# One ring of weight pieces 4096 bytes apart, instead of six buffers 4160 bytes apart

## The reference

```python
for l in range(DEPTH):
    h = rmsnorm(x, pre_norm_g[l])
    proj = h @ w_in[l]                      # 1024 x 10,432
    ...
    merged = (sigmoid(g_a) * (y_a @ w_proj_a[l]) + sigmoid(g_b) * (y_b @ w_proj_b[l])
              + sigmoid(g_c) * (y_c @ w_proj_c[l]))
    x = x + rmsnorm(merged @ w_out[l], post_norm_g[l])
# second block, per layer: pooling or sparse attention, then
    u = h @ w_up                            # 1024 x 5632
    x = x + (silu(g) * a) @ w_down          # 2816 x 1024
    x = x + sigmoid(rmsnorm(x) @ ple_gate[i]) * (p[i] @ ple_proj[i])
```

## Time and profile before

| | |
|---|---|
| median of 3 runs | 1482.29 us (1480.97 to 1482.8) |
| the profiled execution, its own time | 1483.7 us |
| its span, first to last instruction | 1481.9 us |
| TensorE busy | 1437.0 us, 97% |
| TensorE weight loads | 1292.4 us, 87% |
| VectorE busy | 1055.7 us, 71% |
| ScalarE busy | 871.8 us, 59% |
| mean granted TensorE clock | 0.988 of full speed |

### The profile page before, as it was taken

How to read it: one execution, slowest core, us unless ns; L and a number is a source line. 1 busy time by engine, 2 the same in 40 slices (tenths; PEclk the granted TensorE clock), 3 DMA queues, 4 the chain that set the end, 5 groups by cost and what they waited for, 6 DMA issues and landing times.

```text
span 1481.9 us, 23062 instructions
## 1 busy us (share of the span) xinstructions
PE 1437.0 (97%) x9283; PEld 1292.4 (87%) x9283; DVE 1055.7 (71%) x1601; ACT 871.8 (59%) x1522; POOL 85.2 (6%) x138
## 2 busy tenths in 40 slices
PE   8999999999999999999999999999999999999997
PEld 8988999788789989897887789998799888999886
DVE  7736669886666456698876778884676645888746
ACT  7464766564454657575644656664674543766645
POOL 9100000007000000000000000000000000000000
PEclk9999999999999999999999999999999989999999
DMA  8614476556556244765665446665535003666553
GB/s 256 187 47 150 132 225 196 173 186 198 191 144 173 76 144 120 214 186 175 193 220 184 157 132 215 207 205 187 170 103 159 29 1 106 206 186 188 190 178 114
DMA packets 189210, 240.98 MB, mean 163 GB/s; under 512 B 19086, under 2 KB 133954, under 8 KB 189104
## 3 DMA queue, kind: packets, MB, share of 16 engines
q1 hardware_dynamic: 183232, 228.66, 50.7%
q0 software_dynamic: 5776, 10.82, 2.4%
q10 hardware_dynamic: 96, 0.03, 0.0%
HBM read 238.42 MB, written 1.05 MB: 162 GB/s over the span
## 4 chain that ended last, share of the span: by engine, by line
PE 82%; DVE 8%; ACT 5%; DMA 2%; issue 2%; SPq 0%; DVEq 0%
PE bank L620 24%; PE bank L623 23%; PE bank L624 23%; DVE w_lo L1874 2%; PE bank L837 2%; PE bank L1216 2%; ACT w_hi L1321 1%; DMA raw<-in_w_in 1%; ACT T L1815 1%; DMA raw<-in_mla_w_ukv 1%; DMA raw<-in_w_out 1%; DVE rec L1998 1%; PE bank L1173 1%; PE bank L1130 1%; PE bank L1202 1%
## 5 line engine op out<-in xcount | busy, mean ns | idle before, releaser
L1874 DVE TENSOR_TENSOR w_lo<-raw,w_hi 128x1024 fp32r<-128x1024 f32 (+2 forms) x452 | 520.5, 1172 | 240.3 <-ACT w_hi L1321 236.6
L1321 ACT CAST w_hi<-raw 128x1024 fp32r<-128x1024 f32 (+2 forms) x452 | 450.8, 1008 | 271.5 <-DMA raw<-in_w_in 113.4
L620 PE MATMUL bank<-h_hi,w_hi 128*128 128x256 f32 (+1 forms) x1640 | 458.3, 279 | 9.5 <-issue 4.4
L623 PE MATMUL bank<-h_lo,w_hi 128*128 128x256 f32 (+1 forms) x1640 | 455.4, 278 | 0.0
L624 PE MATMUL bank<-h_hi,w_lo 128*128 128x256 f32 (+1 forms) x1640 | 454.7, 277 | 0.0
L620 PEld LDWEIGHTS bank<-h_hi,w_hi 128*128 128x128 f32 (+1 forms) x1640 | 307.9, 188 | 14.2 <-issue 12.0
L623 PEld LDWEIGHTS bank<-h_lo,w_hi 128*128 128x128 f32 (+1 forms) x1640 | 308.0, 188 | 0.1
L624 PEld LDWEIGHTS bank<-h_hi,w_lo 128*128 128x128 f32 (+1 forms) x1640 | 307.9, 188 | 0.0
L620 PE MATMUL bank<-w_hi,h_hi 128*128 128x512 f32 (+1 forms) x464 | 178.5, 385 | 2.7 <-DVE h_lo L1910 1.7
L623 PE MATMUL bank<-w_lo,h_hi 128*128 128x512 f32 (+1 forms) x464 | 176.7, 381 | 0.0
L624 PE MATMUL bank<-w_hi,h_lo 128*128 128x512 f32 (+1 forms) x464 | 176.6, 381 | 0.0
(11 more groups left out here) (366 smaller groups left out, 2133.3 us busy)
## 6 DMA issues: line engine op xcount, KB each, us to landing
raw<-in_w_in SPq DMA_DIRECT2D x160, 512.0 KB, 3.8
raw<-in_ffn_up SPq DMA_DIRECT2D x88, 512.0 KB, 3.7
raw<-in_ffn_down SPq DMA_DIRECT2D x40, 512.0 KB, 4.5
raw<-in_w_proj_a SPq DMA_DIRECT2D x16, 512.0 KB, 3.5
raw<-in_w_proj_b SPq DMA_DIRECT2D x16, 512.0 KB, 3.6
raw<-in_w_proj_c SPq DMA_DIRECT2D x16, 512.0 KB, 3.8
raw<-in_w_out SPq DMA_DIRECT2D x16, 512.0 KB, 3.6
raw<-in_ple_gate SPq DMA_DIRECT2D x16, 512.0 KB, 4.5
```

The costliest lines, as they stand in the source:

```text
L620: first = pe.matmul(out_, lh, rh, start=start, stop=False)
L623: pe.matmul(out_, lh, rl, start=False, stop=False)
L1321: act.copy(weights(w_hi, slot, b, size), weights(raw, slot, b, size)).then_inc(sems["hi_done"], 1)
L1874: dve.tensor_tensor(weights(w_lo, slot, b, size), weights(raw, slot, b, size), weights(w_hi, slot, b, size).bitcast(F32), ALU.subtract).th ...
```

## The change

The six buffers of each kind become one tensor of 6 x 1024 values with a small tail. Piece p lies at place b, which is b x 4096 bytes in, plus 64 bytes where the weights are stationary (k = 3 or 8) and plus nothing where they move. A function at build time walks through the pieces, takes the next place, and leaves one out where the new piece would overlap the piece before it. It also notes for each piece the latest older piece that shares bytes with it (`BEHIND`), and the load waits for that one.

```diff
-def landed(piece):
-    return 16 * sum(2 if SLOTS[p // 2] == (3, 2 * QKD) else 1 for p in range(piece % RING, piece + 1, RING))
...
+def ring_places():
+
+    where, behind = [], []
+    for piece in range(2 * len(SLOTS)):
+        k, n = SLOTS[piece // 2]
+        k0, k1 = halves(k)[piece % 2]
+        b = (where[-1][0] + 1) % RING if where else 0
+        for b in (b, (b + 1) % RING):
+            first = b * PIECE + place(piece // 2)
+            end = first + (k1 - k0) * n
+            if not where or not (first < where[-1][2] and where[-1][1] < end):
+                break
+        older = [p for p, (_, f, e) in enumerate(where) if first < e and f < end]
+        where.append((b, first, end))
+        behind.append(older[-1] if older else None)
+    return where, behind
+
+WHERE, BEHIND = ring_places()
+
+def landed(piece):
+    return 16 * sum(2 if SLOTS[p // 2] == (3, 2 * QKD) else 1 for p in range(piece + 1) if WHERE[p][0] == WHERE[piece][0])
...
-        w_hi = [sb(f"w_hi{b}", [P, PIECE + SHIFT], F32R) for b in range(RING)]
-        landing = overlay([(f"raw{b}", [P, PIECE + SHIFT], F32) for b in range(RING)])
-        raw = [landing[f"raw{b}"] for b in range(RING)]
-        w_lo = [sb(f"w_lo{b}", [P, PIECE + SHIFT], F32R) for b in range(RING)]
+        w_hi = sb("w_hi", [P, RING * PIECE + P], F32R)
+        raw = overlay([("raw", [P, RING * PIECE + SHIFT], F32)])["raw"]
+        w_lo = sb("w_lo", [P, RING * PIECE + 2 * SHIFT], F32R)
...
-            return piece, piece % RING, (k1 - k0) * SLOTS[slot][1]
+            return piece, WHERE[piece][0], (k1 - k0) * SLOTS[slot][1]
...
-            first = place(slot) if b % 2 == 0 else SHIFT - place(slot)
-            return t[b][:, first:first + size]
+            first = b * PIECE + place(slot)
+            return t[:, first:first + size]
...
-                    if piece >= RING:
-                        sp.wait_ge(sems["w_begun"], piece - RING + 2)
+                    if BEHIND[piece] is not None:
+                        sp.wait_ge(sems["w_begun"], BEHIND[piece] + 2)
...
-                    sp.wait_ge(sems["w_begun"], piece - RING + 2)
+                    sp.wait_ge(sems["w_begun"], BEHIND[piece] + 2)
```

## The result

The changed kernel takes 1504.39 us (median of 4 runs, 1503.72 to 1505.99) and the kernel before 1481.63 us beside it: a ratio of 1.0165, with a 95% interval from 1.0138 to 1.0191. By the two medians it is 22.8 us slower. The forecast was 9.0 us faster, and its range ended at 1490.

What follows compares the result with a forecast made beforehand. It took the distance between TensorE matmuls, plus pauses at stage ends, as the bound. Terms of -8.0 - 0.5 - 1.0 + 0.5 = -9.0 us brought 1482.3 to 1473.3 us, range 1468 to 1490.

Steps and rivals of the forecast that it cites:

- Moving weights (-8.0): 2496 matmuls moving 512-column weights, all at 224 modulo 512: distance falls from 230.8 towards 226.7 ns, gaining 8.0 us.
- two signs that the prediction named for being wrong: ffn_down at 230 ns or above; stages differing between stationary activation at 224 (`h`) and at 352 (`y`).
- moving weights lock into the pace of buffer 4: Rival: 512-column moving weights settle at 233.3 ns, 6.2 us slower, 1488 us in all; chance 0.10.
- Everything else (0): Tensors behind the weights move from 480 to 352; waits, instructions and DMA sizes keep their number; priced at nothing, left open.
- Stationary weights (-1.0): 5232 stationary-weight matmuls, all weights at 288: fewer at the slow 118.8 ns instead of 113.3, gaining 1.0 us.
- first rival: Stationary streams lock into the slow pace without alternating addresses: 24 us more, 1498 us in all; chance 0.12.
- The pooling slot (-0.5): Pooling's 144 matmuls, whose weights move, go from 117.8 to some 114 ns without alternation, gaining 0.5 us.
- Loads (+0.5): 31 of 452 pieces load 12 matmuls, 2.8 us, later but stay nearly hidden: cost 0.5 us, at most 5 us.
- The late-pieces rival: Rival: the later loads show and cost 5 us, shrinking the gain to 4.5, 1477.8 us in all; chance 0.03.
- the addresses do nothing: Rival: differences between buffers come from something running along with the ring and stay; 1482.8 us in all; chance 0.15.

Runs made afterwards that it cites:

- e2: Changed kernel with every weight at 288, moving ones too, no load waiting longer, tensors behind the weights still at 352: 1488.19 us, ratio 1.0055 to the kernel before.
- e4: Changed kernel with only the tensors behind the weights put back at 480, by 128 bytes of padding: 1494.08 us, ratio 1.0096 to the kernel before.
- e10: The changed kernel as it is, measured again on one chip beside e9: 1503.74 us, ratio 1.0118 to the kernel before.
- e7: e4 with the low parts of stationary weights at 416, 128 bytes behind the high parts, same late loads: 1492.06 us, ratio 1.0066 to the kernel before.
- e5: Changed kernel with places 4224 bytes apart, no late loads; modulo 256, moving weights at 224, stationary high part at 224, low at 96: 1486.56 us, ratio 1.0042.
- e6: e5 with the two parts of the stationary weights exchanged, high at 96 and low at 224 modulo 256: 1488.04 us, ratio 1.0038 to the kernel before.
- e3: Changed kernel with every weight at 224, the tensors behind them at 480, no load waiting longer: 1488.57 us, ratio 1.0067 to the kernel before.
- e9: Changed kernel with old waits, places 4224 bytes apart, other tensors at 480; modulo 256, moving weights at 224, stationary at 32 and 160: 1476.08 us, ratio 0.9943.
- e1: Kernel before with its own buffers and addresses, but the changed kernel's load waits, 31 loads waiting for one more piece: 1498.53 us, ratio 1.0112.

## Why the prediction was wrong, step by step

**Moving weights (-8.0): right for half of them.** The step took the moving address alone. Where the stationary operand is `h`, at 224, the distance fell from 231.0 to 227.2 on the mean and gave 5.0 us. That half nearly met the upper bound of the step, 4.1 ns off each. Where the stationary operand lies at 352, the distance rose from 230.8 to 232.6, and cost 2.2 us. What counts is the pair of addresses: 224 and 224, or 224 and 480, give 227.0 to 227.2 on the mean in every kernel that has them; 224 and 352 give 232.4 and 232.6, and in e2 288 with 224 gives 229.7 and 288 with 352 gives 233.4. As far as 224 and 480 show, only the address modulo 256 matters. This answers two signs that the prediction named for being wrong: ffn_down is above 230 ns, and stages with `h` and with `y` differ. The rival "moving weights lock into the pace of buffer 4" came true for the half with the stationary operand at 352, but not for its reason: it blamed the stationary address 224, and with that one the pace is the best.

**Everything else (0): the step that lost that half.** The prediction noted that 352 is not 256 bytes away from 224 and priced it at nothing. By e4, which moves only these tensors, it was worth 288.9 - 281.9 = 7.0 us.

**Stationary weights (-1.0): wrong sign, the first rival's mechanism.** Taken over all 5232 matmuls the pace rose by 12.3 us, and in e10 by 18.0. The fast pace of 113.3 and the slow one of 117.8 both still exist; what the change moved is how often a stream is in the slow one. Counting a product of three matmuls as slow when it takes over 345 ns, about 13% are slow before, 66% after, 50% in e4 and 4% in e7, and e7 differs from e4 only by the 128 bytes between high and low part. The low part's new distance to the moving operand, 192 bytes modulo 256, doesn't do it by itself: in the changed kernel `queries` has all stationary parts at 288 and `c` moving at 352, the same 192, and in its first stage every product is slow, 118.2 ns on the mean. So the alternation did release the slow pace, as the rival said. But e5 and e6 alternate too, at 0 and 128 bytes from the moving operand instead of 64 and 192, and stay at 119.1 and 118.4, so the distance to the moving operand matters as well. The rival's price of 24 us was too high: the stream is not slow everywhere, and a slower stream has fewer pauses. In e3 the pace costs 36.1 us and 15.9 of them come back as shorter pauses, in e10 10.8 of 18.0. In this stage of the kernel before, such a pause stands after every 192 matmuls. The trace puts it down to issue, that is, it shows nothing that TensorE waited for:

```profile
929.82 0.28 PE L624 MATMUL bank<-h_hi,w_lo 128*128 128x256 f32 x1
930.39 0.36 PE L620 MATMUL bank<-h_hi,w_hi 128*128 128x256 f32 x1 [0.29 <-issue]
```

Net of the pauses the stationary streams cost 11.3 us in the changed kernel's profile and 7.2 in e10's.

**The pooling slot (-0.5): did not come, and the step had its addresses and its count wrong.** Its moving weights are at 288 in the changed kernel, as shown above, and the slot has 16 calls; the other 32 of the 48 are `tokens` with 256 columns, ahead of the second block's attention, with k = 8 as well. The alternation of the moving input is gone all the same, and the pace stayed at 117.8. So the alternation was not what held this stream above 113.3, and the prediction had built on that. The pace is about 117.8 in e2 (288) and also in e5, e7 and e9, where the weights alternate, and 119.8 to 120.0 in e3 (224) and e6. In e4 the pooling has the same addresses as in the changed kernel and runs at the fast pace, 3.07 us for the 27 distances of the earlier trace rows, while the other 96 matmuls are at 117.8:

```profile
848.68 0.28 PE L640 MATMUL bank<-w_hi,h_hi 128*128 128x256 f32 x1
...
851.75 0.28 PE L640 MATMUL bank<-w_hi,h_hi 128*128 128x256 f32 x1
```

So a stream of 256 columns was seen at two paces at equal addresses, here as in the stationary stream.

**Loads (+0.5): the largest error.** e1 prices it at 16.6 us by its ratio, and e7 against e9, which have the same paces but ran on two chips, at 1.0066 - 0.9943 = 1.2%, 18 us. The step said that the load starts "12 matmuls later, 2.8 us", and it took the cover of 7.2 us from piece 58, in the middle of a smooth stage. Both fail at the end of a layer. There `tokens_in_turn` uses the same pieces twice, once for each half of the tokens, and all but the first count as begun in the second pass only. The load of piece 133 used to wait until piece 128, the first of them, was begun, and now waits until piece 129 is, which is 30 matmuls later. It is issued 9.9 us later than before, of which some 3.0 us is the lag of the stage as a whole (its last matmul starts at 420.51, and before at 417.56). Load issues, the changed kernel first and then the kernel before:

```profile
417.08 0.37 SPq L410 DMA_DIRECT2D raw<-in_w_in  x1
```

```profile
407.14 0.37 SPq L390 DMA_DIRECT2D raw<-in_w_in  x1
```

The piece itself is not needed yet. What is late is what stands behind its rounding in ScalarE's order: `G`, which takes the finished half of the tokens out of PSUM and opens the chain of the norm. In the kernel before it runs at 412.47, during the second pass, and that pass hides the whole chain: the transposes start at 417.79 without a wait. In the changed kernel ScalarE stands 5.89 us for the load, `G` comes at 421.88 when the second pass is over, and TensorE idles 6.46 us:

```profile
410.89 1.05 ACT L1321 CAST w_hi<-raw 128x1024 fp32r<-128x1024 f32 x1 [1.61 <-DMA raw<-in_w_in]
412.47 0.60 ACT L1339 ACTIVATE G<-bank 128x512 f32<-128x512 f32 x1 [0.53 <-PE bank L624]
...
417.79 1.04 PE L745 MATMUL bank<-cst,G 128*128 128x128 f32 x8
```

```profile
413.99 1.05 ACT L1341 CAST w_hi<-raw 128x1024 fp32r<-128x1024 f32 x1 [3.24 <-DMA raw<-in_w_in]
420.93 1.04 ACT L1341 CAST w_hi<-raw 128x1024 fp32r<-128x1024 f32 x1 [5.89 <-DMA raw<-in_w_in]
421.88 0.59 ACT L1359 ACTIVATE G<-bank 128x512 f32<-128x512 f32 x1
...
426.72 0.88 DVE L1914 TENSOR_SCALAR G<-x,st 128x512 f32<-128x512 f32 x2
427.36 1.94 PE L765 MATMUL bank<-cst,G 128*128 128x128 f32 x8 [6.46 <-DVE G L1914]
```

There is a second loss beside the idle time, a lower clock at its end and behind it. In the windows of the changed kernel the granted clock is 1.00 from 421 to 424 us, 0.53 from 424 to 431, of which 0.50 from 426 on, and eight transposes take 1.94 us instead of 1.04; the kernel before has 0.76 over the same 7 us of its own time, so it has such a stretch too, but a shorter one and not under these transposes (the columns are us, busy time and count of the five engines, granted clock, DMA share, GB/s):

```profile
424.00:431.00 7.00, 3.64 (x17) 3.67 (x18) 5.00 (x13) 4.23 (x13) 0.00 (x0) 0.53 0.01 3
```

The same happens ahead of the attention of the second block, where ScalarE waits 5.58 us and TensorE 6.82, and the granted clock is 0.50 from 1091 to 1096 us:

```profile
1083.30 1.05 ACT L1341 CAST w_hi<-raw 128x1024 fp32r<-128x1024 f32 x1 [5.58 <-DMA raw<-in_w_kv]
...
1091.50 3.65 PE L765 MATMUL bank<-cst,G 128*128 128x128 f32 x16 [6.82 <-DVE G L1914]
```

The late-pieces rival had the right place (ScalarE's order, then the banks) and a price of 5 us, a third of what it was. It had been sized by bank waits of 1 us, and not by the chain behind the evacuation.

**The sum.** In the profiled execution 11.3 us come from the stationary streams, net, -5.0 and +2.2 from the moving weights, and 6.7 + 5.8 from pauses and the rest: 21.0. The last two are near what e1 shows with the waits alone (6.8 + 8.2). Against the forecast, the moving weights gave 2.8 us instead of 8.0, the stationary streams cost 11.3 instead of giving 1.0, and pauses and the rest, which hold the loads and also the changing clock, cost 12.5 instead of 0.5.

**The rival "the addresses do nothing"** is out: e4 against the changed kernel and e7 against e4 each change an address and nothing else, and a pace with it.

**Open.** Why the addresses of two operands modulo 256 set the pace, and what puts a stationary stream into one pace or the other, no run shows. The relation to the other operand doesn't explain the alternating buffers of the earlier trace rows either: modulo 256, buffers 1 and 2 had the high part, two matmuls of three, 128 bytes from `y` and took 228.3 and 229.2 ns, while buffers 3 and 4 had only the low part there and took 232.5 and 233.3. How the cost of the late loads divides into the wait itself and the lower clock behind it is not separated; half-clock stretches also come and go between executions (from 1193 to 1206 us the granted clock is 0.50 in the kernel before and 1.00 in e2), and the column "rest" moves by 7 us without late loads: -7.5 in e2, whose mean granted clock is 0.994, and +1.7 in e6 with 0.986, where the kernel before has 0.988. The two ratios of the changed kernel (1.0165 and 1.0118) fit together only at the ends of their intervals.

## What to carry to other kernels

When a float32r stream bounds the kernel, take the distances between starts for each pair of operand addresses modulo 256, and move neither operand without the other: a tensor that only lies behind the one edited counts as moved (ffn_down ran at 233.3 ns with it at 352, at 226.8 with it at 480). A wait for one more buffer is priced where buffers are used twice and at the ends of stages, not in a smooth stretch, and the price is what stands behind the waiting instruction on its engine: here ScalarE waited 5.89 us ahead of `G`, and TensorE 6.46 us for what follows `G`. The slack of a piece, 7.2 us for piece 58, did not show that. The places that let pieces of two kinds overlap cost about 17 us in waits here; e9 gets the good addresses with the old waits for 1024 bytes more of each partition than the kernel before.

## What the hardware showed that was not expected

- Paces that depend on the operands' addresses modulo 256: for a moving float32r stream of 512 columns 226.9 ns (equal addresses), about 230.8 on the mean (alternating, before) and 233.3 (ffn_down with 224 and 352); for a stationary one with 256 columns 113.3, 117.8 and 120.0.
- At equal addresses a stream of 256 columns was at 113.3 or at 117.8 ns: 93 distances at the one, then a pause of 0.45 us and 94 at the other in one stage of the changed kernel, and 189 in a row at 117.8 in e2 and e4. A pause isn't needed for it: in the changed kernel the pace falls from 117.8 to 113.3 at 1352.51 us, where the longest distance is 0.13 us.
- With both operands at 224 modulo 256 the stream of 512 columns has its best pace, 226.9, and the one of 256 columns its worst, 120.0 (e3).
- Over the last 3.4 us of an idle time of 6.5 us on TensorE and the 3.6 us behind it the granted clock was 0.53, and eight transposes took 1.94 us instead of 1.04.
